# Scheduling the first expert tiles of a two-layer diffusion backbone: a ring of four buffers in layer 1, early tiles split around the gate building, eight early tiles in layer 0

## The reference

```python
def chunk(h):                                    # 128 tokens
    q = (h @ wq).reshape(t, PEER_HEADS, 2, PEER_DQ // 2)
    s = jnp.einsum('thpd,hpnd->thpn', q, sub_keys)
    sv, si = lax.top_k(s, PEER_TOPK)             # 16 of 128, twice
    cand_s = sv[:, :, 0, :, None] + sv[:, :, 1, None, :]
    cand_i = si[:, :, 0, :, None] * PEER_NKEYS + si[:, :, 1, None, :]
    best_s, best = lax.top_k(cand_s, PEER_TOPK)  # the choices, 16 per head
    idx = take_along_axis(cand_i, best)
    gate = softmax(best_s)
    act = gelu(einsum('td,thkd->thk', h, u[idx]))
    return einsum('thk,thkd->td', gate * act, v[idx])
x = layer_norm(ALPHA * x + gate_mod * y)
```

## Time and profile before

| | before |
|---|---|
| median of 3 runs | 3264.99 us (3264.13 to 3265.53) |
| the profiled execution: its own time, its span | 3266.49 us, 3264.7 us |
| PE busy (share of the span) | 2932.0 us (90%) |
| DVE, ACT, POOL busy | 2125.9, 1192.8, 538.2 us |
| mean DMA rate over the span | 191 GB/s |

### The profile page before, as it was taken

The page is one execution under the profiler, slowest core; times in us unless marked ns, Lnnn a source line. Parts: engine busy times, 40 slices in busy tenths (PEclk is TensorE's granted clock), DMA queues, the critical chain, the costliest instruction groups (busy, mean ns, idle before and its releaser), DMA issues.

```text
span 3264.7 us, 44619 instructions
## 1 busy us (share of the span) xinstructions
PE 2932.0 (90%) x15829; PEld 2441.4 (75%) x15829; DVE 2125.9 (65%) x3872; ACT 1192.8 (37%) x2059; POOL 538.2 (16%) x341
## 2 busy tenths in 40 slices
PE   7799996797777999999999999689777699999997
PEld 1488884481476999999999999565676579999997
DVE  0165563489995777777777777644579666656566
ACT  0222220221493333333333333213336544444443
POOL 0000000221001333333333333100552000000000
PEclk9899997898898999999999999799899899999999
DMA  6311102324478878777878788420444766655654
GB/s 260 149 65 64 64 26 77 129 78 187 152 203 281 275 277 274 273 278 272 284 271 283 268 280 273 167 110 1 154 145 145 226 238 207 211 208 210 216 202 148
DMA packets 223240, 623.17 MB, mean 191 GB/s; under 512 B 16264, under 2 KB 104496, under 8 KB 216880
## 3 DMA queue, kind: packets, MB, share of 16 engines
q1 hardware_dynamic: 186300, 487.99, 42.8%
q0 software_dynamic: 36864, 134.23, 12.2%
HBM read 570.68 MB, written 51.48 MB: 191 GB/s over the span
## 4 chain that ended last, share of the span: by engine, by line
PE 73%; DVE 14%; DMA 5%; issue 2%; ACT 2%; POOL 1%; DVEq 1%; SPq 0%; ACTq 0%; POOLq 0%
PE bank L910 26%; PE bank L953 25%; PE bank L738 5%; PE bank L833 3%; PE bank L867 2%; DVE arena L1653 2%; PE bank L780 2%; DVE arena L1654 2%; PE bank L745 2%; PE bank L703 2%; DMA arena<-in_wst 1%; DMA arena<-in_u 1%; POOL u_lo L1861 1%; DMA arena<-in_v 1%; PE bank L994 1%
## 5 line engine op out<-in xcount | busy, mean ns | idle before, releaser
L910 PE MATMUL bank<-h_parts,u_hi 128*128 128x384 f32 (+1 forms) x4096 | 905.5, 312 | 45.0 <-POOL u_lo L1861 25.5
L953 PE MATMUL bank<-v_parts,p_hi 128*128 128x512 f32 x2560 | 798.6, 393 | 23.9 <-DVE p_lo L1679 23.7
L910 PEld LDWEIGHTS bank<-h_parts,u_hi 128*128 128x128 f32 x4096 | 707.0, 192 | 66.1 <-issue 46.5
L910 PE MATMUL bank<-h_parts,u_lo 128*128 128x384 f32 (+1 forms) x2048 | 637.9, 311 | 0.0
L953 PEld LDWEIGHTS bank<-v_parts,p_hi 128*128 128x128 f32 x2560 | 472.7, 189 | 118.9 <-issue 16.2
L953 PE MATMUL bank<-v_parts,p_lo 128*128 128x512 f32 x1280 | 502.1, 392 | 0.0
L1675 DVE TENSOR_TENSOR arena<-arena 128x384 f32<-128x384 f32 (+1 forms) x256 | 190.4, 744 | 422.7 <-ACT arena L1283 400.9
L1283 ACT ACTIVATE arena<-bank 128x384 f32<-128x384 f32 (+1 forms) x232 | 102.9, 443 | 905.7 <-PE bank L910 905.7
L910 PEld LDWEIGHTS bank<-h_parts,u_lo 128*128 128x128 f32 x2048 | 392.4, 192 | 0.0
L1677 DVE TENSOR_TENSOR v_parts<-arena,v_parts 128x1024 fp32r<-128x1024 f32 x256 | 313.7, 1225 | 63.0 <-ACT v_parts L1286 55.0
L1658 DVE TENSOR_TENSOR u_lo<-arena,u_hi 128x1024 fp32r<-128x1024 f32 x232 | 283.4, 1222 | 89.5 <-ACT u_hi L1200 72.8
(11 more groups left out here) (224 smaller groups left out, 3580.0 us busy)
## 6 DMA issues: line engine op xcount, KB each, us to landing
arena<-in_u SPq DMA_DIRECT2D x256, 512.0 KB, 4.5
arena<-in_v SPq DMA_DIRECT2D x256, 512.0 KB, 3.6
arena<-in_wst SPq DMA_DIRECT2D x39, 2048.0 KB, 7.6
gate_scratch<-arena SPq DMA_DIRECT2D x20, 2048.0 KB, 8.7
arena<-gate_scratch SPq DMA_DIRECT2D x32, 768.0 KB, 5.0
arena<-in_whd SPq DMA_DIRECT2D x8, 2560.0 KB, 9.1
arena<-gate_scratch SPq DMA_DIRECT2D x32, 512.0 KB, 4.5
x_scratch<-arena SPq DMA_DIRECT2D x10, 512.0 KB, 3.0
```

The costliest lines, as they stand in the source:

```text
L910: last = mm(banks[q][:, 0:ND[p]], w[:, q, col], h[:, k, DS[p]], start=(n3 == 0), stop=(n3 == 3 * KT - 1))
L953: last = mm(banks[2 + 2 * b + half][:, :], x[:, q, b * P:(b + 1) * P], y[:, q, col], start=(first and i == 0), stop=(final and i == 2))
```

## The change

- Layer 1: the early tiles are split. 16 of them (EARLY[1]) come before the gate building, and the other 8 right after it. The 16 use a ring of four buffers: tiles with j % 4 of 2 or 3 use v's buffers (`v_raw`, `v_hi`, `v_lo`) in place of u's.
- Layer 0: KA[0] = 8 and EARLY[0] = 0, so the scores of tiles 0 to 7 come in one block right after the gate building, and the outputs of tiles 0 to 6 behind them. DVE now uses the first 16 gathered rows in this block, four behind each of the low parts of tiles 4 to 7. The low parts of the first four tiles no longer wait until the gates are written.
- Gelus read back from `gelu_scratch` go to a buffer of their own (`act_l`).
- EXP_AFTER = 8: the exponential stands behind the gelu of tile 8.
- SP: gate rows and the first two gelus are loaded in the middle of the new block, the layer-norm rows behind it.

```diff
-EXP_AFTER = 13
-KA = [0, 24]
+KA = [8, 24]
+EARLY = [0, 16]
+EXP_AFTER = 8
...
+        act_l = ar(B_HF + 4096, 768, s=2, t=ND_MAX)
...
# SP
-                for j in range(KA[p]):
-                    sp.wait_ge(u_l[j % 2], 1 + p * PAIRS + j // 2 + 1)
-                    sp.dma_start(u_raw[:, j % 2, :], a["u"][p, j + 2]).then_inc(u_in[j % 2], 16)
+                for j in range(4 if early else 2):
+                    load_u(j)
+                for j in range(early):
+                    sp.wait_ge(u_l[j % 2], 1 + N0 + j // 2 + 1)
+                    if j + 4 < early + 2:
+                        load_u(j + 4)
                     if j:
                         act_store(j - 1)
...
-                gates(0, 0)
-                if KA[p]:
-                    for q in range(2):
-                        sp.wait_ge(act_out[q], 16 * (KA[p] // 2))
-                    for q in range(2):
-                        acts(q, q)
+                for j in range(early, K0):
+                    sp.wait_ge(u_l[j % 2], 1 + N0 + j // 2 + 1)
+                    load_u(j + 2)
+                    if j > early:
+                        act_store(j - 1)
+                    if j == early + 3:
+                        for q in range(2):
+                            sp.wait_ge(g_out[q], 1 + 16 * (GC_BASE[p] + ND[p] // GCH // 2))
+                        gates(0, 0)
+                        for q in range(2):
+                            sp.wait_ge(act_out[q], 16 * (ACT_BASE[p] + 1))
+                            acts(q, q)
+                act_store(K0 - 1)
+                for q in range(2):
+                    sp.wait_ge(act_out[q], 16 * (ACT_BASE[p] + K0 // 2))
                 sp.wait_ge(x_out, 16 * LN_BASE[p])
...
# PE, behind the gate building
-                if K0 == 0:
-                    scores(0, N0)
-                    scores(1, N0)
+                with pe.Fori(early // 2, K0 // 2) as n:
+                    for q in range(2):
+                        scores(q, n + N0)
                 outputs(0, N0, True, False)
...
# ACT
-                if K0:
-                    high_u(0, N0)
-                for j in range(K0):
-                    if j + 1 < K0:
-                        high_u((j + 1) % 2, N0 + (j + 1) // 2)
...
+                for j in range(min(3, early)):
+                    high_early(j)
+                for j in range(early):
+                    if j + 3 < early:
+                        high_early(j + 3)
+                    ahead(j)
                     if j == EXP_AFTER:
                         gate_exponentials()
...
+                high_u(0, N0 + early // 2)
+                for j in range(early, K0):
+                    if j + 1 < K0:
+                        high_u((j + 1) % 2, N0 + (j + 1) // 2)
+                    ahead(j)
+                step(0, N0, 1, N0, more=False, own=False)
...
# DVE
-                for q in range(2):
-                    dve.wait_ge(g_sb[q], 1 + 2 * (G_BASE[p] + ND[p] // 16))
-                    dve.wait_ge(g_out[q], 1 + 16 * (GC_BASE[p] + ND[p] // GCH // 2))
...
+                for j in range(early, K0):
+                    low_u(j % 2, N0 + j // 2)
+                    if j == early + 3:
+                        for q in range(2):
+                            dve.wait_ge(g_sb[q], 1 + 2 * (G_BASE[p] + ND[p] // 16))
+                            dve.wait_ge(g_out[q], 1 + 16 * (GC_BASE[p] + ND[p] // GCH // 2))
+                    if p == 0 and j >= early + 4:
+                        for x in range(4 * (j - early - 4), 4 * (j - early - 3)):
+                            score_row(0, x)
+                if p == 0:
+                    dots_done(0)
+                step(0, 0, N0, gate_in(0, 0), 1, N0, more=False, own=False)
...
# POOL
-                for j in range(KA[p]):
+                for j in range(EARLY[p]):
                     q, N = j % 2, p * PAIRS + j // 2
+                    lo, raw, hi = (u_lo, u_raw, u_hi) if j % 4 < 2 else (v_lo, v_raw, v_hi)
                     pool.wait_ge(u_h[q], N + 1)
```

More of the change, by code:

```diff
@@ L902, in peer, with scores @@
                     mod_columns(mod1, CHUNKS * KT // 2, banks[3])
-                def scores(q, N):
+                def scores(q, N, high=u_hi, low=u_lo):
                     pe.wait_ge(u_l[q], 1 + N + 1)
-                    pe.wait_ge(s_act[q], N)
+                    pe.wait_ge(s_act[q], 1 + N)
                     n3 = 0
@@ L908, in scores @@
                         col = slice(k * P, (k + 1) * P)
-                        for w, h in ((u_hi, h_hi), (u_hi, h_lo), (u_lo, h_hi)):
+                        for w, h in ((high, h_hi), (high, h_lo), (low, h_hi)):
                             last = mm(banks[q][:, 0:ND[p]], w[:, q, col], h[:, k, DS[p]], start=(n3 == 0), stop=(n3 == 3 * KT - 1))
@@ L912, in scores @@
                     last.then_inc(s_pe[q], 1)
-                N0, K0, nB = p * PAIRS, KA[p], KA[p] // 8
-                if K0:
-                    with pe.Fori(0, K0 // 2) as n:
+                N0, K0, nB, early = p * PAIRS, KA[p], KA[p] // 8, EARLY[p]
+                if early:
+                    with pe.Fori(0, early // 4) as n:
                         for q in range(2):
-                            scores(q, n + N0)
+                            scores(q, 2 * n + N0)
+                        for q in range(2):
+                            scores(q, 2 * n + 1 + N0, v_hi, v_lo)
                 for n in range(nd):
@@ L1297, in peer @@
                     act.wait_ge(g_pe[q], 1 + 2 * (G_BASE[p] + ND[p] // 16))
-                if K0:
-                    step(0, N0, 1, N0, more=False, own=False)
+                high_u(0, N0 + early // 2)
[4 more added lines that the diff above has]
+                step(0, N0, 1, N0, more=False, own=False)
+                if nB > 1:
                     with act.Fori(0, nB - 1) as n:
                         steps8(n, True)
-                    steps8(nB - 1, True)
-                else:
-                    high_u(0, N0)
-                    step(0, N0, 1, N0)
+                steps8(nB - 1, True)
                 if p == 0:
```

98 lines of the change are left out of this document (58 added, 40 removed).

## The result

| | before | changed |
|---|---|---|
| median | 3264.13 us (5 runs, 3261.93 to 3265.53) | 3278.26 us (5 runs, 3275.12 to 3281.92) |
| span of the profiled execution | 3264.7 us | 3276.4 us |

The ratio is 1.0042, with a 95% interval of 1.0032 to 1.0053. I had forecast 3270 us, within a range of 3255 to 3280. The measured time lies inside the range only because it reaches up to rival 2, whose time it is; my likeliest case's own range, 3265 to 3275, was missed, and by the medians the change cost 14 us where I had 5.

A forecast was written before the change was run, and what follows sets the result against it. PE was taken as the nearly always busy engine, its gaps set by waits for gates, loads and the exponential. Layer 0 +7 and layer 1 -2 gave +5 on the median 3265: 3270 us, range 3255 to 3280, about 8 in 10.

The forecast's parts named there:

- rival 2: Layer 0: gathers saturate the queue once one takes over 7 us; layer 0 +15, sum +13, 3278 us; chance 0.27.
- my likeliest case: Whole kernel: layer 0 +7 us, layer 1 -2 us, sum +5, 3270 us; own range 3265 to 3275; chance 0.38.
- Start of layer 0: Layer 0: low parts follow the last gate copy at once, so scores(0) starts at 992.7, 8.1 us sooner.
- Rows among the low parts: Layer 0's block: the ring of four gathers sets the pace, about 7 us per four rows; outputs(0) at 1040.6.
- Layer-norm rows behind the block: Layer 0: eight layer-norm loads ahead of tile 2's v make 18 us of queue; outputs(2) starts at 1061.
- Layer 1: Earlier exponential and choices gain 25.8 us, eight tiles behind the gates give back 23.7; net -2 us.
- the late tiles: Layer 1, eight tiles behind the gates: outputs(2) 50.4 us behind the last gate piece, before 26.7; 23.7 us given back.
- T + 12.9: Layer 1: start of tile 18's scores, 12.9 us behind T, when the last gate piece leaves, forecast at 2539.8.
- the split buys nothing that the earlier exponential didn't: Layer 1: splitting the early tiles adds no gain, since PE is idle from 2425 to 2452.
- the forecast of C: Layer 1: first one-hots at 2451.8 instead of 2477.6, with DVE's small operations slowed by POOL, done at 2420.5 instead of 2412.5.
- Rival 1: Both gates open: DVE not slowed by POOL, layer 1 -10, layer 0 near -2; -12, 3253 us; chance 0.27.
- Rival 3: Layer 1: ACT meets the exponential before DVE has shifted the scores, early tiles stall; +6, sum +11, 3276 us; chance 0.08.

The follow-up runs named there:

- run 6: The changed kernel with EXP_AFTER = 13 again, so the exponential is late; 3283.56 us, ratio 1.0054 to the kernel before.
- run 3: The changed kernel with the layer-norm rows of both layers loaded one at a time among the last six tiles' loads; 3261.98 us, ratio 0.9995.
- Run 2: The changed kernel with no gathered row used in layer 0's block, all 16 used in the steps that follow; 3266.60 us, ratio 1.0010.
- run 4: The changed kernel with no gathered row used in layer 0's block and the layer-norm rows late in both layers; 3245.57 us, ratio 0.9937.
- run 5: The kernel before with only the layer-norm rows loaded late, in both layers; 3250.59 us, ratio 0.9963.
- run 1: The changed kernel with layer 0 as before and layer 1 still changed; 3262.95 us, ratio 0.9998 to the kernel before.
- Run 7: The kernel before with EXP_AFTER = 8 alone, so the exponential is early; 3266.23 us, ratio 1.0002.
- run 10: The changed kernel with layer 0 as before and, in layer 1, 16 early tiles and none behind the gates; 3258.30 us, ratio 0.9975.
- run 8: The changed kernel with layer 0 as before and, in layer 1, all 24 early tiles ahead of the gates in the ring of four; 3252.53 us, ratio 0.9964.
- run 11: The kernel before with layer 0's low parts of tiles 0 and 1 ahead of the wait for the gates; 3263.71 us, ratio 0.9994.
- run 12: Changed kernel, layer 0 without early tiles, 24 before layer 1's gates, layer-norm rows late, low parts of tiles 0 and 1 before the gate wait; 3232.44 us, ratio 0.9897.

## Why the prediction was right or wrong, step by step

**Start of layer 0: right.** Scores(0) was forecast 2.3 us behind the last gate piece and came at 990.67, 2.3 behind it.

**Rows among the low parts: mechanism right, size wrong.** This is the term that failed: "four rows take 5.3 + 0.3 for the issue + 1.2 for the row, about 7 us". They took 10.3 and 9.0 us; in the two other traces of the same block 10.7 and 11.1 (run 6), 9.2 and 7.8 (run 3), so all six are over 7. The loop itself is as I wrote it, from the use of row 7 to that of row 11; POOL's timeline shows the two gathers that close it:

```profile
1028.40 1.68 POOL L1922 DMA_INDIRECT arena<-in_ug,arena  x1 [0.60 <-DVE arena L1733]
...
1038.69 1.68 POOL L1922 DMA_INDIRECT arena<-in_ug,arena  x1 [3.48 <-DVE arena L1733]
```

But a gather landed 8.75 and 7.4 us after its issue, not 5.3. The 5.3 of the earlier trace rows is a median over all 256 gathers of u and v, nearly all from the steady rhythm, where two rows are used per tile; in the block four gathers and a tile load meet in each 10 us. Counted from the gate piece, scores(6) came at +41.0 (forecast +34.3), scores(7) at +51.2 (+41.4), outputs(0) at +61.8 (+50.2). Of these 11.6 us, 3.6 were there before the first row was used (tile 2's load landed 1.3 us later than I had it, and tile 4's took 7.45 us); 3.1, 3.1 and 1.8 came with rows 4 to 7, 8 to 11 and 12 to 15. I had the condition in rival 2, "as soon as a gather takes over 7 us", and saw the 13.7 us of the earlier trace rows; for a burst, the upper part of the row was the better estimate. Run 2 shows what all waits on the rows cost, 16.2 us in A. With both waits gone the block is level with the old one (76.3 in run 4, 75.4 in run 5), so of layer 0's 18.7 us about 16 are the rows and about 3 the new place of the layer-norm rows (an estimate from runs 2, 3 and 5).

**Layer-norm rows behind the block: right.** From outputs(0) to outputs(2) 20.4 us were forecast and 21.2 measured. Runs 3 and 5 show that the same eight loads cost 12 us in their old place and 15 in the new. That a score and an output covered them there and outputs alone here is how I explain the 3 us; it was not tested by itself.

**Layer 1: right to 2 us.** The gain was forecast at 25.8 us and came at 26.8, the late tiles at 23.7 and came at 24.4, the net at -2 and came at -1.5; run 1, with layer 0 as before, is 1.5 us under the kernel before, which its interval can't tell from nothing. One sum in it was wrong: from scores(18) at T + 12.9, six scores of 2.87 and the 2 and 1.5 us of losses add to T + 33.6, not to T + 32.2. Scores(23) ended 34.1 us behind the gate piece, and the store (1.72 us) and the v load were quicker than I had them, so that outputs(2) still came within 1 us of the forecast: there the sum was helped by luck.

**What I had wrong in layer 1 without its showing in the sum.** I wrote "the split buys nothing that the earlier exponential didn't". Run 7 shows that the earlier exponential alone buys nothing, since 24 tiles in two buffers keep PE until 2476. Run 6 shows that the ring of four and 16 tiles together, without the earlier exponential, bring 24.9 of the 26.8 us. And the eight tiles behind the gates are a loss either way: without them it is 5 us faster (run 10 against 1), with them ahead of the gates 10 (run 8 against 1).

**POOL and DVE.** The Trainium skill, "SBUF — State Buffer", section "Who interferes with whom", has a DVE instruction with two SBUF inputs and a GpSimd instruction that reads SBUF exclude each other for the whole instruction. The trace after agrees: L1649 takes 2.53 us beside a low part on POOL and its sibling L1648 0.42, and in run 8 a pair L1690 takes 8.79 us beside POOL and 4.49 without. With 16 tiles the forecast of C that allows for it was 1 us off; run 8 against run 10, which differ ahead of the gates in nothing but eight more tiles, puts the price of those at 14.4 us.

**Rivals.** Rival 1 fell (DVE was slowed, no gap was open). Rival 2 came true in direction and size: the condition that it named, a gather over 7 us, was met, scores(7) ended 58.4 us behind the gate piece (forecast 1045, which is 54.6) and layer 0 came at +18.7 (forecast +15). Its mechanism, a queue at its limit, is likely and not shown (below). Rival 3 fell: the exponential ran at 2422.0 and held nobody.

**Left open.** Why a gather lands in 7 to 9 us in the block was not measured by itself; that the transfers are at 322 GB/s speaks for plain queueing. No run used another ring size or moved the tile loads, so a slower gather for another reason isn't ruled out. The bound of run 12 in layer 1 was not looked into.

## What to carry to other kernels

Before a wait is moved or removed, list all chains that end within a few us of it: here the exponential and the early tiles ended together, and the earlier exponential alone was worth nothing (run 7); so was the earlier start of layer 0 (run 11), and with the loads behind it moved too it took 2.4 us off A (run 12). Look first at what is in the transfer queue ahead of the first loads of a stage: loads that are needed a thousand us later stood there, and moving them won 14 us with no new buffer. Take a transfer's time for a burst from the slow end of its row, not from a median over the steady stage.

## What the runs showed of the hardware

PE's granted clock was 0.70 over the second half of the block, where PE was busy for 25.5 of 40 us in pieces between waits, and 0.96 over the first, where PE's waits up to 1022.8 were of 1.2 to 3.0 us.

What an idle time costs the next score is not one number here. A score takes 4.18 us in the rhythm and took 7.19 behind 8.5 us of idle time (its line stands in run 11); for scores(0), behind 3 us, I had taken half of the difference, which is 5.7 us, and it took 5.9 (990.67 to 996.5). But scores(7), behind 3.03 us, took 7.22 us (1039.61), and in the two other traces of the same block 6.04 behind 4.04 us (run 6) and 6.03 behind 3.29 us (run 3). Scores(6) took 7.2 us behind 6.65 there, 6.6 behind 8.09 (run 6) and 5.9 behind 6.38 (run 3). So behind 3 to 8 us the surcharge lay between 1.7 and 3.0 us, not in the order of the idle times, and these traces don't say what decides it.

DVE and POOL stretched each other in layer 1: a pair of DVE's instructions took 8.79 us beside POOL's low parts and 4.49 us without them (run 8).
